# Mixture-of-experts passes in another order: the smallest expert second, a full pass between the mixed ones, the pass table in two parts, mixed pieces in pairs

## What is computed

```python
def moe_swiglu(h, w_router, wg, wu, wd):
    logits = (h @ w_router).astype(jnp.float32)
    top_v, top_i = lax.top_k(logits, TOP_K)
    top_w = jax.nn.softmax(top_v, axis=-1)
    gates = jnp.einsum('blk,blke->ble', top_w, jax.nn.one_hot(top_i, N_EXPERTS, dtype=jnp.float32)).astype(h.dtype)
    y = jnp.zeros_like(h)
    for e in range(N_EXPERTS):
        y = y + gates[..., e:e + 1] * swiglu(h, wg[e], wu[e], wd[e])
    return y
```

## Time and profile before

| | us |
|---|---|
| median of 3 runs | 1383.92 |
| the runs | 1381.20, 1383.92, 1388.71 |
| the profiled execution, its time | 1383.09 |
| its span from first to last instruction | 1381.2 |
| its mean granted TensorE clock | 0.965 of 2.4 GHz |

### The profile page before, as it was taken

The page is one execution under the profiler, slowest core; times in us unless marked ns, Lnnn a source line. Parts: engine busy times, 40 slices in busy tenths (PEclk is TensorE's granted clock), DMA queues, the critical chain, the costliest instruction groups (busy, mean ns, idle before and its releaser), DMA issues.

```text
span 1381.2 us, 17263 instructions
## 1 busy us (share of the span) xinstructions
PE 1300.3 (94%) x6503; PEld 959.1 (69%) x6504; DVE 718.9 (52%) x1021; ACT 525.1 (38%) x632; POOL 120.5 (9%) x119
## 2 busy tenths in 40 slices
PE   5999999999999999999999799999789999999994
PEld 2555459999999854776558686654356778888882
DVE  1101565342432426554246874623335668898888
ACT  0101043332422232332125463522324557777772
POOL 0510005000000051000000000101002010202020
PEclk8999999999999999999996899999998999999997
DMA  9985474443342375511216774768966879999993
GB/s 366 359 323 214 174 283 138 153 164 109 108 165 91 117 277 179 211 33 70 98 67 232 242 247 162 255 244 317 367 233 213 310 281 378 368 371 392 372 352 150
DMA packets 125355, 317.09 MB, mean 230 GB/s; under 512 B 12931, under 2 KB 47078, under 8 KB 124774
## 3 DMA queue, kind: packets, MB, share of 16 engines
q1 hardware_dynamic: 119264, 295.00, 58.3%
q0 software_dynamic: 5744, 21.07, 5.0%
q10 hardware_dynamic: 278, 0.10, 0.0%
HBM read 306.37 MB, written 9.76 MB: 229 GB/s over the span
## 4 chain that ended last, share of the span: by engine, by line
PE 82%; DMA 7%; DVE 6%; SPq 2%; ACT 2%; issue 1%; DVEq 0%; ACTq 0%
PE ps L2526 9%; PE ps L2528 8%; PE ps L2527 8%; PE ps L2224 8%; PE ps L2226 8%; PE ps L2225 8%; PE ps L2189 7%; PE ps L2126 6%; PE ps L2532 5%; DMA sb_expert_raw<-in_moe_w_up 4%; PE ps L2316 3%; DVE sb_expert_w L1755 2%; DMA sb_ring<-in_ev_w_in 2%; PE ps L2086 2%; PE ps L2418 1%
## 5 line engine op out<-in xcount | busy, mean ns | idle before, releaser
L1755 DVE TENSOR_TENSOR sb_expert_w<-sb_expert_raw,sb_expert_w 128x1792 fp32r<-128x1792 f32 (+1 forms) x210 | 339.0, 1648 | 130.4 <-ACT sb_expert_w L1204 129.6
L1204 ACT CAST sb_expert_w<-sb_expert_raw 128x1792 fp32r<-128x1792 f32 (+1 forms) x210 | 287.1, 1392 | 178.9 <-DMA sb_expert_raw<-in_moe_w_down 88.4
L2526 PE MATMUL ps<-sb_expert_w,sb_expert_x 128*128 128x448 f32 x448 | 171.9, 384 | 27.5 <-DVE sb_expert_w L1755 16.7
L2527 PE MATMUL ps<-sb_expert_w,sb_expert_x 128*128 128x448 f32 x448 | 166.9, 373 | 0.0
L2528 PE MATMUL ps<-sb_expert_w,sb_expert_x 128*128 128x448 f32 x448 | 166.8, 372 | 0.0
L2526 PEld LDWEIGHTS ps<-sb_expert_w,sb_expert_x 128*128 128x128 f32 x448 | 86.5, 193 | 57.6 <-issue 34.2
L2224 PE MATMUL ps<-sb_split_acts,sb_split_weights 128*128 128x384 f32 x352 | 118.7, 337 | 0.4 <-issue 0.4
L2226 PE MATMUL ps<-sb_split_acts,sb_split_weights 128*128 128x384 f32 x352 | 118.4, 336 | 0.0
L2225 PE MATMUL ps<-sb_split_acts,sb_split_weights 128*128 128x384 f32 x352 | 118.4, 336 | 0.0
L2528 PEld LDWEIGHTS ps<-sb_expert_w,sb_expert_x 128*128 128x128 f32 x448 | 86.3, 193 | 7.7
L2527 PEld LDWEIGHTS ps<-sb_expert_w,sb_expert_x 128*128 128x128 f32 x448 | 86.6, 193 | 7.1
(11 more groups left out here) (334 smaller groups left out, 1830.5 us busy)
## 6 DMA issues: line engine op xcount, KB each, us to landing
sb_expert_raw<-in_moe_w_gate SPq DMA_DIRECT2D x128, 448.0 KB, 6.4
sb_expert_raw<-in_moe_w_up SPq DMA_DIRECT2D x128, 448.0 KB, 7.7
sb_expert_raw<-in_moe_w_down SPq DMA_DIRECT2D x112, 512.0 KB, 5.1
sb_ring<-in_ada_w SPq DMA_DIRECT2D x14, 3072.0 KB, 17.0
sb_ring<-in_ffn_w_gate SPq DMA_DIRECT2D x44, 256.0 KB, 3.7
sb_ring<-in_ffn_w_up SPq DMA_DIRECT2D x44, 256.0 KB, 4.7
sb_ring<-in_ffn_w_down SPq DMA_DIRECT2D x22, 512.0 KB, 6.2
sb_ring<-in_ev_w_in SPq DMA_DIRECT2D x4, 2048.0 KB, 14.9
```

What stands on the lines that cost most here:

```text
L1204: nc.scalar.copy(EWS[r][:, 0, 0:w], ERAW[:, r, 0:w]).then_inc(e_hi, 1)
L1755: V.tensor_tensor(EWS[r][:, 1, 0:w], ERAW[:, r, 0:w], EWS[r][:, 0, 0:w].bitcast(F32), ALU.subtract)\
L2526: first = mm(out, lh, rh, start=start, stop=False)
L2527: mm(out, lh, rl, start=False, stop=False)
```

## The change

1. `PASSES` is reordered: ranks 0, 1 (mixed half), 7 (whole), 2 (mixed quarter), 5, 6, 3 become 0, 7 (whole), 1 (mixed half), 3, 2 (mixed quarter), 5, 6.
2. The table is made in two parts. `by_pass` writes only the experts of the static passes in pass 0 and releases the engines (`order_ready`); `left_over` and `passes_of` move to the start of pass 1 on DVE, and `more_items` moves behind the static passes on every engine.
3. `turn_at` puts ACT's and DVE's handling of the transposed hidden rows of the pass behind the whole-weight pass at piece 15 and no longer at 17.
4. In mixed passes PE takes two pieces for the first block, then the same two for the second block, where it alternated piece by piece.

```diff
 PASSES = (
     (0, full(), None),
+    (7, half(), None),
     (1, full(), more_half(P)),
-    (7, half(), None),
+    (3, full(), None),
     (2, full(), more_quarter(P)),
     (5, full(), None),
     (6, full(), None),
-    (3, full(), None),
 )
...
+        def turn_at(p, before):
+
+
+            return KD + EB if before in WHOLE else KD + spread(before) + 4
+
...
+        def order_ready(eng):
+
+            eng.wait_ge(tab_ready, 1)
+
         def more_items(eng):
 
-            eng.wait_ge(tab_ready, 1)
+            eng.wait_ge(tab_ready, 2)
...
             def pass_highs(p, before):
 
-                turn = KD + spread(before) + 4
+                turn = turn_at(p, before)
                 expert_highs(p, 0, KD + 4)
                 gate_silu(p, 0)
                 expert_highs(p, KD + 4, turn)
                 h_high(p, 0)
                 expert_highs(p, turn, KD + EB + 4)
                 y_out(before)
-                expert_highs(p, KD + EB + 4, 2 * KD + EB + 4)
+                expert_highs(p, max(turn, KD + EB + 4), 2 * KD + EB + 4)
...
+            def by_pass():
+
+                ch(V.tensor_tensor(above, across(IX[:, 0:NE]), down_(cst("iota", 1)[:, 0:NE]), ALU.is_equal))
+                ch(V.tensor_tensor(above, above, across(cst("iota", 1)[:, 0:NE]), ALU.mult))
+                ch(V.tensor_reduce(FIRST, above, AX.X, ALU.add))
+                V.tensor_copy(TAB[:, 1:1 + NE], FIRST).then_inc(tab_ready, 1)
+
             def left_over():
 
+                by_rank(CAP, "rows_of")
...
+                passes_of(0, cand("cand_expert"))
+                passes_of(1, FROM)
+                V.tensor_copy(TAB[:, 0:1], TF[:, 0:1])
+                V.tensor_copy(TAB[:, 1 + NE:], TF[:, 1 + NE:]).then_inc(tab_ready, 1)
...
             def pass_lows(p, before):
 
                 after = p + 1 if isinstance(p, int) else (p[0], p[1] + 1)
-                turn = KD + spread(before) + 4
+                turn = turn_at(p, before)
                 expert_lows(p, 0, 4)
+                if p == 1:
+                    left_over()
                 select(after)
...
             by_rank(IX[:, 0:NE], "pass_of")
-            by_rank(CAP, "rows_of")
-            expert_lows(0, 4, 5)
-            left_over()
-            expert_lows(0, 5, 6)
+            by_pass()
+            order_ready(dve)
+            expert_lows(0, 4, 6)
             dve.wait_ge(h_stored, 16 * NG)
-            passes_of(0, cand("cand_expert"))
             expert_lows(0, 6, 7)
-            passes_of(1, FROM)
-            V.tensor_copy(TAB[:, :], TF).then_inc(tab_ready, 1)
-            more = more_items(dve)
             picked(0)
             select(1)
...
+                for k in range(0, KD, 2):
+                    primary(k)
+                    primary(k + 1)
                     if more_rows:
-                        if k == 0 and u == 0:
-                            tokens_split(pe, p, 1)
-                        elif k == 0:
-                            hidden_split(pe, p, 0, 1)
-                        _, last = gate_up_block(more_rows, XES2, piece.r, k)
-                        if k == KD - 1:
-                            last.then_inc(gu_ps, 1)
-                    if k < KD - 1:
-                        last.then_inc(e_used, 1)
+                        secondary(k)
+                        secondary(k + 1)
...
-                for j in range(spread(p), EB):
-                    primary(j)
+                for j in range(spread(p), EB, 2):
+                    pair = range(j, min(j + 2, EB))
+                    for i in pair:
+                        primary(i)
                     if more_rows:
-                        secondary(j)
+                        for i in pair:
+                            secondary(i)
```

More of the change, by code:

```diff
@@ L786, in _ @@
                 expert_down(e_piece(0, 2 * KD + b), 0, b)
-            more = more_items(sp)
+            order_ready(sp)
             def pass_loads(p, e_before, e):
@@ L803, in _ @@
                 e_before = e
+            more = more_items(sp)
             with sp.Fori(0, more) as j:
@@ L961, in _ @@
             pool.wait_ge(h_stored, 16 * NG)
-            more = more_items(pool)
             n = 0
@@ L969, in _ @@
                     n += 1 + (p - 1 in SECOND)
+            more = more_items(pool)
             with pool.Fori(0, more) as j:
@@ L1807, in _ @@
             row = lambda a, n: MS[0:1, a:a + n]
+            FIRST = row(800, 8)
             KEY, RANK, IX, CAP, STARTS, FROM = row(300, 8), row(308, 8), row(316, CANDS), row(340, 8), row(348, 16), row(364, CANDS)
@@ L1969, in _ @@
                 pass_lows(p, p - 1)
+            more = more_items(dve)
             per = 6
@@ L2575, in gate_up, with primary @@
                 x = XEW if p in WHOLE else XES
-                for k in range(KD):
+                def primary(k):
                     piece = e_piece(p, c0 + k)
@@ L2583, in gate_up, with secondary @@
                         last.then_inc(gu_ps, 1)
-                    if more_rows:
-                        if k == 0 and u == 0:
-                            tokens_split(pe, p, 1)
-                        elif k == 0:
-                            hidden_split(pe, p, 0, 1)
-                        _, last = gate_up_block(more_rows, XES2, piece.r, k)
-                        if k == KD - 1:
-                            last.then_inc(gu_ps, 1)
-                    if k < KD - 1:
-                        last.then_inc(e_used, 1)
+                    elif not more_rows:
+                        last.then_inc(e_used, 1)
+                def secondary(k):
+                    if k == 0 and u == 0:
+                        tokens_split(pe, p, 1)
+                    elif k == 0:
+                        hidden_split(pe, p, 0, 1)
+                    _, last = gate_up_block(more_rows, XES2, e_piece(p, c0 + k).r, k)
+                    last.then_inc(gu_ps if k == KD - 1 else e_used, 1)
+                for k in range(0, KD, 2):
+                    primary(k)
+                    primary(k + 1)
+                    if more_rows:
+                        secondary(k)
+                        secondary(k + 1)
             def down_block(b, h, col, r, start, stop):
@@ L2691, in _ @@
             gate_up(0, 0, 0, False)
-            more = more_items(pe)
+            order_ready(pe)
             pick(1)
@@ L2704, in _ @@
                 pass_products(p, p - 1)
+            more = more_items(pe)
             with pe.Fori(0, more) as j:
```

## The result

The changed kernel takes 1374.94 us (median; 1369.7 to 1380.59) beside 1383.51 for the kernel before on the same chip: ratio 0.9947, 95% interval 0.993 to 0.9964. That is 8.6 us less, where 24 were forecast, and it lies just above the range. The profiled execution has a span of 1372.2 us, at a mean granted clock of 0.964 (before: 1381.2 and 0.965).

What follows compares the result with a forecast made beforehand. PE bounds the mixed half pass, transfers the whole-weight pass. 8.3 us in pass 0, 6.5 by pairs, 4.6 by hidden rows and 4 to 5 by order take 24.1 off the median 1383.92: 1360, range 1351 to 1374.

Steps and rivals of the forecast that it cites:

- The table: Pass 0: the table in two parts removes PE's 5.44 us wait for DVE and 1.45 of slow clock.
- the shorter pick and turns: End of pass 0: six pick matmuls in place of twelve, 0.7 us off; token turns lose about as much.
- The whole-weight pass: Pass 1: 17.4 MB at 399 GB/s take 43.7 us, so pass 2 starts at 865.3; the pass lasts 53.2.
- Rival 1: Slow transfers throughout the whole-weight pass, 349 GB/s: 6.2 us more, 1366; chance 0.16.
- The hidden rows: Second gate and up unit of pass 2: earlier copy leaves 4.2 of the 8.8 us wait; 4.6 gained.
- The pairs: Mixed passes: fewer block changes save 1.3 us per gate and up unit, 0.65 per half-pass down unit; 6.5 entered.
- rival 2: Pairs give nothing and hold slots: 6.5 us lost and four waits of 1.4, 1372; chance 0.10.
- The order: The new order of passes brings the rest of the gain, 4 to 5 us.
- 1 for small waits: Pass 3, full: 1 us of waits within its 70.1, as transfers and PE are almost level.
- Passes 4 and 5: Mixed quarter pass 4 takes 87.0 us, with 1.2 of wait; full pass 5 behind it takes 71.7.
- Rivals 3 and 4: Table edit fails or delays pass 1: 7 us, 1367, chance 0.07; pass 1's clock stays 1.2 GHz: 1402, chance 0.04.
- three signs of being wrong: DMA under 380 GB/s in pass 1; new waits above 2 us in passes 3 or 5; clock under 0.9 in pass 1.

Runs made afterwards that it cites:

- e1: The kernel before with only the new order of passes, without the other three edits: 1383.31 us, ratio 1.0008.
- e9: Changed kernel reordered: full, mixed half, full, mixed quarter, whole, full, full; adds of passes 1 and 3 held back by one pass: 1367.27 us.
- e7: Changed kernel without the first expert's add, and fetching 32 of 1024 columns of the token rows for pass 2 (wrong rows): 1366.61 us.
- e5: Changed kernel with the hidden rows of the pass behind the whole-weight pass turned as late as before: 1377.55 us.
- e4: Changed kernel without pairs, the two blocks taking turns piece by piece as before: 1376.28 us.
- e8: Changed kernel in the old order of passes, the two adds of mixed pass 1 held until PE is in the quarter pass: 1365.65 us.
- e11: As e8 (old order, late adds) but without the pairs: 1367.27 us.
- e10: As e8 (old order, late adds) but with pairs in the half pass alone: 1367.7 us.
- e3: Changed kernel with GpSimd's adds of passes 0 and 2 held until PE is in the mixed pass behind: 1370.51 us.
- e2: Changed kernel with the old order of passes, keeping the table in two parts, earlier turn and pairs: 1370.18 us.
- e6: Changed kernel without the first expert's add into the sums, 8 columns written to spare rows instead: 1373.17 us.

## Why the prediction was wrong, point by point

**The table: right.** PE's wait of 5.44 and the twelve matmuls of the pick are gone; the changed kernel shows six and a turn that waits as before:

```profile
773.50 0.73 PE L2519 MATMUL ps<-sb_scratch,sb_temp 128*128 x6
777.13 1.76 PE L2683 MATMUL ps<-sb_constants,sb_scratch 128*128 128x128 f32 x7 [2.90 <-DVE sb_scratch L1923]
```

In the twelve profiled executions with the split table (this one's and those of all experiments but e1) pass 1 starts between 807.6 and 815.2, mean 812.3; in the two with the old table (before and e1) it starts at 820.3. That is 8.0, with 8.3 forecast. Read from the first expert matmul to pass 1, which leaves out what differs ahead of it, the old order takes 67.5 with the old table and 60.5 with the new one (mean of six executions, e9's among them, whose pass 1 is the half pass too), the new order 66.1 (e1) and 59.1 (mean of six). So the table gives 7.0 in either order, with 6.9 forecast, and the shorter pick and turns that come with the new order 1.4, with 1.4 forecast. In the time, alone and in the old order, the table was worth 5.9.

**The whole-weight pass: the step that failed.** "At the 399 GB/s of the steadiest stretch under whole-weight work that is 43.7 us." The term counted 17.4 MB of weights and nothing else, and left out that GpSimd's transfers share the engines. Two fetches and one add come into that pass, 1.22 MB in 9 us, and the rate of 399 was read from a stretch, 918 to 938, in which none ran. The row that pointed to the answer was the 349 of the whole-weight pass before, which the prediction put down to pauses behind the mixed down unit. In that pass too PE waited for weights, just behind a fetch and an add that GpSimd issued at 960.19 and 961.43:

```profile
970.41 7.07 PE L2532 MATMUL ps<-sb_expert_raw,sb_whole_x 128*64 128x512 f32 x24 [2.27 <-DMA sb_expert_raw<-in_moe_w_up]
```

The changed kernel's pass moves 349 as well. The pass was 9.4 longer than said; 7.2 of that goes with the indirect traffic (e7: 55.4). The other 2.2 no run takes away. They fit the chain from slot to slot: a transfer can't start before PE has left the piece six before, so a stream of pieces isn't at its full rate in the first units, where PE is the slower one (in e7 315 GB/s over the first unit and 353 over the second). Rival 1 had the right rate and the right place with another cause, and at 6.2 us it was still too small; the wait inside the pass brought the slow clock (0.59 for 4.2 us) on top, which it didn't count.

**The hidden rows: right in mechanism and size, not in what stays.** The wait left over is 4.51, with 4.2 forecast, and e5 gives 8.78 without the edit. Of the 4.3 taken away, 2.6 are left between the medians.

**The pairs: right on the spot, wrong in the sum.** Two pieces of the half pass with both their blocks take 8.64, start to start, in place of twice 4.50:

```profile
884.86 0.47 PE L2547 MATMUL ps<-sb_expert_w,sb_expert_x 128*128 128x448 f32 x1
...
889.92 3.65 PE L2553 MATMUL ps<-sb_expert_raw,sb_second_x 128*64 128x512 f32 x16
893.50 0.47 PE L2547 MATMUL ps<-sb_expert_w,sb_expert_x 128*128 128x448 f32 x1
```

That is 0.36 less, where 0.33 was forecast, and 34.6 per unit without waits. But 6.5 was entered as gain, and e4 finds 1.3, e8 against e11 and e10 nothing that can be told from zero. The profiles show it lost again in the passes behind, where PE lives on what lands. The waits there, 2.41 and 2.88 where e4 has 0.34 and 1.76, fit rival 2's mechanism, slots that are freed a block later (it was given 0.10); that it is the slots was not shown by itself.

**The order: wrong sign.** Forecast 4 to 5 less; alone it changes nothing (e1), and on top of the edits it costs 4.8 (1374.94 against 1370.18). The indirect transfers are a part of it: in the new order two fetches and an add fall into the whole-weight pass, and two fetches and two adds into the full pass, where transfers and PE are almost level. But the adds don't make the difference between the orders: with them held back in both, the new order still costs 4.9 between the medians (e3 against e8; the intervals overlap by 0.001). Two stretches of these show where it stands, the full pass between the mixed ones in e3 and its counterpart in e8, pass 5:

```profile
979.20:1050.20 71.00, 70.83 (x349) 57.69 (x348) 57.35 (x54) 48.99 (x39) 5.47 (x4) 1.00 0.88 333
1143.80:1207.20 63.40, 62.41 (x306) 54.72 (x305) 55.18 (x44) 46.94 (x37) 5.51 (x4) 1.00 0.98 367
```

The half pass's last down unit, with its second block, now lies in a full pass that PE bounds (18.8 where a plain one takes 11.2) and no longer in the whole-weight pass, whose transfers covered it. The forecast had this 7.7 in its 70.1. It counted on the whole-weight pass becoming 13.6 shorter in return (66.8 to 53.2), and against e2 it became 6.4 shorter, against e8 in e3 6.3; the half pass behind it grew by 3.9 in both. So the order's sign follows from the term that failed. Whether the fetches, which stay in both orders, cost one more than the other was not tested.

"1 for small waits" in pass 3 was the second half of the same oversight: 5.0 more, of which e3 takes back 4.1 by moving the two adds.

**Passes 4 and 5.** Pass 4 took 2.7 more. Its second unit starts behind a wait of 2.41 with a slow clock after it, where 1.2 was entered; without pairs it is 0.34. Pass 5 came out at 71.6 for 71.7, but with waits of 2.88 and 2.72 at its two units.

**Rivals 3 and 4** didn't come. The clock over pass 1 was 0.95. Of the prediction's three signs of being wrong two showed: 349 GB/s in pass 1, under the 380 (in e7 it is 365, so part of this is not the indirect traffic), and a wait of 2.72 at the second unit of pass 5, where 1.05 stood at that place before.

What stays open: why the saved time of an edit in one pass comes back in the next (2.6 of 4.5, 1.3 of 3.3) was seen in the profiles of e3, e4 and e5 but not taken apart by slot.

## What to carry to other kernels

Count every queue's bytes in a stretch that lives on its transfers, and not the stream alone that you follow: a rate read from a quiet stretch doesn't hold beside a gather or a scatter-add, and a short ring of slots passes a stall on at once. Side transfers that nobody waits for (here the adds into the sums) go beside the work that PE bounds; holding them back was worth 4.4 and 4.5 us in the two orders, as much as half of the whole change, though each by itself is at the edge of its interval. Work that PE bounds is best left in a pass whose transfers cover it. And a saving in a compute-bound pass was a gain here only as far as the pass behind could be fed earlier.

## What the runs showed of the hardware

- An indirect transfer cost the path more than its bytes: in 841 to 850 us 1.22 MB of it held the 16 engines for 49.9% of the time and 1.80 MB of weights for 54.9%, so 3.7 and 2.7 us for each MB; alone, the weights of e7 took 102.0% for 3.62 MB, 2.5 us for each MB.
- While both queues had work (845 to 850 us), each sent 200 packets, and together they moved 270 GB/s; the weights alone moved 405 with e7's small fetches.
- The length of one wait of PE did not by itself say what the granted clock would be behind it: behind 1.81 us in the changed kernel it was 0.72 over 3.5 us, behind 4.38 us 0.59 over 4.2 us, and behind 2.15 us in e6's pass 1 (848.78) it was 1.00 over 4.2 us. In e7's pass 1, with waits of 0.2 to 0.4 before single pieces, it stayed at 1.00. The first and the third of these stretches:

```profile
1037.50:1041.00 3.50, 3.46 (x13) 3.11 (x14) 3.50 (x4) 2.09 (x2) 0.00 (x0) 0.72 1.06 341
848.80:853.00 4.20, 3.85 (x16) 0.95 (x16) 0.00 (x0) 0.00 (x0) 0.00 (x0) 1.00 1.03 407
```
